# Fourteen modulation chunks as VectorE dot products, and the low halves that open the second layer's MLP cut in pieces

## The reference, cut to what matters

```
for layer in range(2):
    mod_x = silu(c) @ ada_w[layer] + ada_b[layer]        # 1024 -> 6144, for the tokens
    mod_c = silu(c_ctx) @ ada_w[layer] + ada_b[layer]    # the same for the context
    sh1, sc1, g1, sh2, sc2, g2 = split(mod_x, 6)
    ...mixer..., x = x + g1 * (mx @ w_out[layer])
    hx = rmsnorm(x, norm2_g[layer]) * (1 + sc2) + sh2
    x = x + g2 * (square(relu(hx @ w_mlp1[layer])) @ w_mlp2[layer])   # 1024 -> 4096 -> 1024
    if layer == 0: the same for ctx, with mod_c
```

## Time and profile before

| | |
|---|---|
| runs | 2018.05, 2015.6 and 2018.36 us, median 2018.05 |
| profiled execution | 2015.12 us by its own clock, of which the span of the profile is 2013.3 us |
| TensorE (PE) | 1929.2 us busy, 96% of the span |
| VectorE (DVE) | 754.5 us, 37% |
| ScalarE (ACT) | 625.2 us, 31% |
| GpSimd (POOL) | 392.5 us, 19% |
| MLP of l = 0, as the span counts | from 1261 to 1592 us |
| MLP of l = 1 | from 1815 us |

### The profile page before, as it was taken

How to read it: one execution, slowest core, us unless ns; L and a number is a source line. 1 busy time by engine, 2 the same in 40 slices (tenths; PEclk the granted TensorE clock), 3 DMA queues, 4 the chain that set the end, 5 groups by cost and what they waited for, 6 DMA issues and landing times.

```text
span 2013.3 us, 27741 instructions
## 1 busy us (share of the span) xinstructions
PE 1929.2 (96%) x11650; PEld 1396.9 (69%) x11650; DVE 754.5 (37%) x1241; ACT 625.2 (31%) x939; POOL 392.5 (19%) x205
## 2 busy tenths in 40 slices
PE   5999999999999999998999899999999999888998
PEld 2777786954444444446887657777777778678998
DVE  1625255632222222225343844222223535564333
ACT  2523113232222222213112534222333511545454
POOL 2000000110000000004002232333333210424664
PEclk9999999989999999998999999999999999999999
DMA  9469817559999999981323004444444223414451
GB/s 359 161 244 363 294 54 298 198 231 414 427 420 424 423 423 426 421 349 51 113 84 126 34 32 146 147 153 171 157 146 146 85 94 116 170 43 163 172 184 47
DMA packets 120215, 428.41 MB, mean 213 GB/s; under 512 B 5690, under 2 KB 23141, under 8 KB 107456
## 3 DMA queue, kind: packets, MB, share of 16 engines
q1 hardware_dynamic: 118016, 416.56, 53.7%
q0 software_dynamic: 2112, 10.57, 1.5%
HBM read 426.07 MB, written 1.05 MB: 212 GB/s over the span
## 4 chain that ended last, share of the span: by engine, by line
PE 64%; PEld 18%; issue 7%; DVE 4%; ACT 3%; POOL 2%; DMA 1%; PEldq 0%; DVEq 0%; POOLq 0%; SPq 0%; ACTq 0%
PE bank L532 62%; PEld bank L532 18%; PE bank L547 2%; DMA ring<-in_ada_w 1%; DVE H L1930 1%; DVE H_low L1937 0%; POOL arena L1845 0%; POOL arena L1844 0%; PEldq L511 0%; DVE arena L2450 0%; POOL arena L1849 0%; POOL arena_r L1885 0%; POOL arena L1847 0%; POOL arena L1850 0%; POOL ring_low L1871 0%
## 5 line engine op out<-in xcount | busy, mean ns | idle before, releaser
L532 PE MATMUL bank<-arena_r 128*128 128x512 f32 (+1 forms) x2304 | 634.3, 345 | 13.6 <-ACT arena_r L1351 5.4
L532 PE MATMUL bank<-arena_r,ring_low 128*128 128x512 f32 (+2 forms) x1920 | 597.2, 343 | 5.4 <-DVE H_low L1937 5.3
L532 PEld LDWEIGHTS bank<-arena_r 128*128 128x128 f32 x2304 | 404.3, 190 | 106.6 <-issue 48.4
L532 PEld LDWEIGHTS bank<-arena_r,ring_low 128*128 128x128 f32 (+1 forms) x1920 | 353.5, 189 | 51.4 <-issue 6.1
L532 PE MATMUL bank<-arena 128*128 128x64 bf16 (+8 forms) x2588 | 304.0, 282 | 26.8 <-DMA arena<-in_hy_filt_w 11.5
L532 PE MATMUL bank<-ring,arena 128*64 128x512 f32 x1024 | 278.2, 595 | 1.1 <-ACT arena L1531 0.7
L532 PEld LDWEIGHTS bank<-arena 128*128 128x128 bf16 (+4 forms) x2588 | 187.1, 131 | 129.6 <-issue 94.7
L532 PE MATMUL bank<-H_low,arena_r 128*128 128x512 f32 (+1 forms) x672 | 216.3, 339 | 0.0
L2508 DVE SCALAR_TENSOR_TENSOR X<-bank,mod,X 128x256 f32<-128x256 f32 x216 | 94.6, 479 | 316.9 <-PE bank L532 316.7
L1871 POOL TENSOR_TENSOR ring_low<-ring,arena_r 128x2048 fp32r<-128x2048 f32 x32 | 146.9, 4613 | 137.7 <-ACT arena_r L1721 70.1
L1365 ACT ACTIVATE arena<-bank 128x512 f32<-128x512 f32 (+2 forms) x106 | 51.2, 496 | 373.2 <-PE bank L532 373.0
(11 more groups left out here) (297 smaller groups left out, 1940.3 us busy)
## 6 DMA issues: line engine op xcount, KB each, us to landing
ring<-in_moe_w_gate SPq DMA_DIRECT2D x32, 2048.0 KB, 13.9
ring<-in_w_mlp SPq DMA_DIRECT2D x32, 2048.0 KB, 8.7
ring<-in_w_in SPq DMA_DIRECT2D x26, 2048.0 KB, 8.1
ring<-in_ada_w SPq DMA_DIRECT2D x24, 2048.0 KB, 11.9
ring<-in_moe_w_up SPq DMA_DIRECT2D x17, 2048.0 KB, 9.5
H<-in_moe_w_down SPq DMA_DIRECT2D x16, 2048.0 KB, 16.3
arena<-in_moe_w_up SPq DMA_DIRECT2D x15, 2048.0 KB, 9.6
ring<-in_moe_w_down SPq DMA_DIRECT2D x15, 2048.0 KB, 16.5
```

Of the source, the lines that this page charges most:

```text
L532: ins = nc.tensor.matmul(o, l, r, start=start, stop=stop, skip_group_check=True)
```

## The change

Part A is in the MLP of l = 0. The first step's pair of modulation chunks stays on TensorE. The other seven pairs, 42 blocks of 128 output columns, are computed on VectorE. Their weights come transposed (`ada_t_2`: 128 columns on the partitions, 1024 inputs along the free axis, 3 blocks to a chunk), and `CSIL` holds silu(c) and silu(c_ctx) spread over all partitions, 128 x 2048. It is brought by a GpSimd DMA, and ScalarE applies the silu behind step 0. For each block VectorE multiplies the 128x1024 weights by each of the two vectors and sums along the free axis into a column of `mod`: 12 instructions in a step, 84 in all. Three turns of four are gone, and the bias is added once behind the last step. TensorE now waits for `dots` between the hid phase and the W2 phase, and the W1 slot and both modulation slots are freed there together.

Part B is at the opening of l = 1's MLP. The second piece of W1's low half moves from GpSimd to VectorE, behind its second add. The high copy of W2 moves on ScalarE from behind the norm to between the squares of tiles 3 and 4. The low half of W2 is made in two pieces of 2048, the first ahead of the norm and the second behind it.

```diff
+                                if isinstance(i, int) and h == 0:
+                                    load(n, cols(T["ada_w_2"][1], q * ADA_COLS, ADA_COLS), as_cols(n, ADA_COLS), i * per)
+                                else:
+                                    load(n, rows(T["ada_t_2"], q * ADA_COLS, ADA_COLS), as_turned(n), i * per)
...
-                        chunk_used(3 if early else 1)
-                        n += 1
-                        if early:
-                            n += 2
-                        elif l == 0:
-                            for a in range(2):
-                                ada(n, 7 + i, 7, 2 * u + a, 4, ADA_COLS, turns)
-                                n += 1
+                        if l == 0 and not early:
+                            pe.wait_ge(S("dots"), 6 * j)
+                        chunk_used(1 if l else 3)
+                        n += 1 if l else 3
                         pe.wait_ge(S("w_split"), 9 + 8 * l + j + 1)
...
-                            if (l, u, nt) == (0, 1, 3):
-                                ada_turn(7 + i, 7, 0, 4, ADA_COLS)
+                            if (l, j, nt) == (0, 0, 3):
+                                ada_turn(7, 7, 0, 2, ADA_COLS)
...
                     square(k, W).then_inc(S("squares"), 1)
+                    if l and k == 3:
+                        act.wait_ge(full[(MLP1 + 1) % RING], arrived(MLP1 + 1))
+                        A_(W2h, slot(MLP1 + 1), ACT.Copy).then_inc(S("w_high"), 1)
...
+                        if l == 0 and isinstance(i, int) and u == 0:
+                            ada_rows(7, 7, 0, ADA_COLS)
+                            act.wait_ge(S("b2_in"), 16 * 5)
+                            A_(CSIL, CSIL, ACT.Silu).then_inc(S("silu_c"), 1)
...
-                low_w1(0, 0)
+                low_w1(0, 0, range(2 - l))
                 add_squares(4 + 2 * l, W)
                 phase_end(pool, f"l{l}_out")
+                if l == 0:
+                    bring(CSIL, T["c_all_2"].rearrange("p (a d) -> p a d", a=2), "b2_in")
...
                     add(t, ps[OUT_BANK[t]], 16).then_inc(S("w_out_added"), 1)
+                    if l and t == 1:
+                        dve.wait_ge(S("w_high"), 24 + 2)
+                        V.tensor_tensor(low(MLP1)[:, 2048:4096], slot(MLP1)[:, 2048:4096], W1h[:, 2048:4096].bitcast(F32), ALU.subtract)\
+                            .then_inc(S("w1_split"), 1)
...
+                if l:
+                    dve.wait_ge(S("w_high"), 24 + 3)
+                    low_w2(MLP1 + 1, 0, 2048)
                 norm(ncall, 1 + l, 1, (0, 1) if l == 0 else (0,))
...
+                        dotted = l == 0 and not (isinstance(i, int) and (i, u) == (0, 0))
+                        if dotted:
+                            dve.wait_ge(S("silu_c"), 2)
+                            dots(i, u, range(4))
                         dve.wait_ge(S("w_high"), 24 * l + (i * 2 + u) * 3 + 3)
                         n = mlp_chunks(l, u, 1, i)[0]
-                        V.tensor_tensor(low(n), slot(n), W2h.bitcast(F32), ALU.subtract).then_inc(S("w_split"), 1)
+                        low_w2(n, 2048 if l and isinstance(i, int) and (i, u) == (0, 0) else 0, 4096).then_inc(S("w_split"), 1)
+                        if dotted:
+                            dots(i, u, range(4, 6))
...
+                def dots(i, u, blocks):
+                    n0, turns = MLP0 + 4 * u + 1, i * 32
+                    for q in blocks:
+                        n = n0 + q // 3
+                        if q % 3 == 0:
+                            dve.wait_ge(full[n % RING], arrived(n) + turns)
+                        if q or not (isinstance(i, int) and (i, u) == (0, 1)):
+                            dve.wait_ge(S("dots"), i * 12 + u * 6 + q - 6)
+                        for c in range(2):
+                            d = V.scalar_tensor_tensor(CPROD[:, c, :], as_turned(n)[:, q % 3, :], 1.0, CSIL[:, c, :], ALU.mult, ALU.mult,
+                                                       accum_out=mod[:, 2, bass.ds(i * 12 + u * 6 + q, 1), c])
+                        d.then_inc(S("dots"), 1)
...
+                    dve.wait_ge(S("ada_out"), 2 + 8)
+                    dve.wait_ge(S("dots"), 42)
+                    lo = VOFF["ada_b2"][0] + 48
+                    link(V.tensor_tensor(mod[:, 2, 6:48, :], mod[:, 2, 6:48, :], bc(vecs[:, lo + 6:lo + 48].unsqueeze(2), [P, 42, 2]), ALU.add))
                     gains(2)
```

More of the change, by code:

```diff
@@ L252, in as_rows, with as_turned @@
             return slot(n).rearrange("p (k n) -> p k n", k=4)
+        def as_turned(n):
+            return slot(n)[:, 0:3 * D].rearrange("p (b d) -> p b d", b=3)
         E5 = 8328 + 3 * 4096
@@ L344, in _, with mlp_loads @@
                     load(first + 16 + j, cols(T["w_out_2"][l], j * 512, 512), as_cols(first + 16 + j))
-                with sp.Fori(0, 4) as i:
+                def mlp_loads(i):
                     n = mlp
@@ L357, in _ @@
                         n += 1
+                if l == 0:
+                    mlp_loads(0)
+                with sp.Fori(1 - l, 4) as i:
+                    mlp_loads(i)
             for a in range(4):
@@ L492, in build @@
         MLP_BANK = (4, 5, 2, 3)
+        CSIL, CPROD = A3(12288, 2, D), A3(22944, 2, D)
         W1h_cols, W2h_rows = W1h.rearrange("p (k n) -> p k n", k=KT), W2h.rearrange("p (k n) -> p k n", k=4)
@@ L873, in _ @@
                        "logits" if (tb, k) == (1, 7) else None)
-            pe.wait_ge(S("sw_zero"), 1)
+            pe.wait_ge(S("selected"), 1)
             pe.wait_ge(S("h_rest"), 4)
@@ L880, in _ @@
                 stat(2, k, L, CSQ)
-            pe.wait_ge(S("selected"), 1)
+            pe.wait_ge(S("selected"), 2)
             mm(ps[5][:, 0:NX], SLT, SELX[:, 0, :])
@@ L1742, in mlp_pair @@
                             high_w1(n)
[L1743 to L1746, removed]
+                        if not (l and isinstance(i, int) and u == 0):
+                            n, turns, chunks, back = mlp_chunks(l, u, 1, i)
+                            act.wait_ge(full[n % RING], arrived(n) + turns)
+                            act.wait_ge(used, n - back + 1 + chunks)
+                            A_(W2h, slot(n), ACT.Copy).then_inc(S("w_high"), 1)
                         for nt in range(4):
@@ L1852, in _ @@
                 pool.wait_ge(S("lgam"), l + 1)
-                pool.wait_ge(S("b2_in"), 16 * (4 + l))
+                pool.wait_ge(S("b2_in"), 16 * (4 + 2 * l))
                 head_args(0)
@@ L1864, in _, with low_w1 @@
                 phase_end(pool, f"l{l}_att")
-                def low_w1(i, u):
+                def low_w1(i, u, halves=range(2)):
                     n = mlp_chunks(l, u, 0, i)[0]
-                    for a in range(2):
+                    for a in halves:
                         s = slice(2048 * a, 2048 * (a + 1))
@@ L2526, in _, with low_w2 @@
                 phase_end(dve, f"l{l}_out")
+                def low_w2(n, a, b):
+                    return V.tensor_tensor(low(n)[:, a:b], slot(n)[:, a:b], W2h[:, a:b].bitcast(F32), ALU.subtract)
+                if l:
+                    dve.wait_ge(S("w_high"), 24 + 3)
+                    low_w2(MLP1 + 1, 0, 2048)
                 norm(ncall, 1 + l, 1, (0, 1) if l == 0 else (0,))
@@ L2538, in mlp_pair @@
                             add(t, ps[MLP_BANK[t % 4]], 40).then_inc(S("mlp_bank_free"), 1)
-                            if (l, u, t) == (0, 1, 4):
-                                take_chunk(2, 7 + i, 7, i * 12, 4, ADA_COLS)
+                            if l == 0 and not dotted and t == 4:
+                                take_chunk(2, 7, 7, 0, 2, ADA_COLS)
                             if l == 0 and closing and t in (2, 3):
@@ L2547, in mlp_pair @@
                                     i_.then_inc(full[(L1 + 1) % RING], 16)
-                with dve.Fori(0, 3) as i:
+                def dots(i, u, blocks):
[10 more added lines that the diff above has]
+                        d.then_inc(S("dots"), 1)
+                mlp_pair(0)
+                with dve.Fori(1, 3) as i:
                     mlp_pair(i)
@@ L2580, with spread @@
         arrays[name] = I[name]
+    def spread(v):
+        return np.broadcast_to(v.reshape(1, -1), (P, v.size))
+    arrays["ada_t_2"] = np.ascontiguousarray(I["ada_w_2"][1].T)
+    arrays["c_all_2"] = np.ascontiguousarray(spread(np.concatenate([I["c_2"].reshape(-1), I["c_ctx_2"].reshape(-1)])))
     arrays["wr"] = np.concatenate([I["moe_router_g_w"][0], I["moe_router_e_w"][0].transpose(1, 0, 2).reshape(D, NX)], axis=1)
```

18 lines of the change are left out of this document (7 added, 11 removed).

## The result

The changed kernel takes 2022.68 us (median of 20 runs), the kernel before 2018.09 us (20 runs): a ratio of 1.0027 with the interval 1.0018 to 1.0036. It is slower by 0.27%, about 5 us. The range held the time, but the forecast, no change with a lean to faster, did not hold.

A forecast was written before the change was run, and what follows sets the result against it. TensorE was taken to bound the kernel (89% of the chain). Part A −21.4 + 17.5 + 5.1 + 0.3 = +1.5 and part B −1.9 summed to −0.4 us: 2014.7 by profile, 2017.7 by median, given as 2017, range 2005 to 2028.

The forecast's parts named there:

- no change with a lean to faster: Whole kernel: 2017 us; chances 0.38 within 0.2% of before, 0.35 faster, 0.27 slower.
- What goes from TensorE, −21.4 us: MLP of l = 0: seven modulation pairs (19.7 us) and three turns (1.7 us) leave TensorE's list.
- the bias included that I put at +0.3: End of the MLP of l = 0: the bias over 84 columns costs some 0.3 us.
- The pause, 2.5 us a step, +17.5: Between hid and W2 phase, seven steps: TensorE waits for dots ending 24.6 us after hid phase start H; bounds 0 to 27.
- The rate of the dot products: VectorE, MLP of l = 0: 1222 ns per 128x1024 instruction, readout of the sum 0 to 160 ns.
- The half-rate rival: VectorE's dot instructions: with a sum they take twice the time, 2.29 us; +87 us, about 2105; chance 0.04.
- The clock, three falls, +5.1: Behind the new TensorE pauses in l = 0: clock falls three times in seven, 1.7 us each; bounds 0 to 11.9.
- The rival with a fall in every pause: MLP of l = 0: seven falls of 1.7 us, stall 2.8 to 3.3 us; about 2026 to 2030; chance 0.23.
- The ring: W1's slot in l = 0 comes free later, leaving 0.4 us of slack before the hid phase; costed at nothing.
- Part B, −1.9: Opening of l = 1's MLP: shorter first-step wait and no fall there, longer pause ahead of opening; −1.9 us (−4 to 0).
- VectorE's piece was charged with 0.4 us: Opening of l = 1's MLP: VectorE's piece may be held by GpSimd's, costing 0.4 us.

The follow-up runs named there:

- late_behind: Changed kernel, TensorE's wait for dots moved behind three W2 part tiles, VectorE's last four dot instructions held until GpSimd's third subtraction; 1993.10 us, 0.9876 of before.
- The kernel with one input: Changed kernel, each dot instruction replaced by a tensor-scalar sum over the weights alone, reading one SBUF input (different modulation); 1994.39 us, 0.9885 of before.
- filler: Changed kernel plus nine unused 128x512 matmuls on TensorE before its wait for dots, in steps 1 to 7 of l = 0; 2014.75 us, 0.9987 of before.
- drop1: Changed kernel with the last of a step's twelve dot instructions cut from 1024 to 64 columns; 2005.46 us, 0.9938 of before.
- the late wait: Also late_wait: changed kernel, TensorE waits for dots only behind the first two W2 part tiles; 1999.92 us, 0.9909 of before.
- part B alone: Part B put on the kernel before, modulation left as it was; 2016.59 us, 0.9995 of before.
- a_only: Changed kernel with part B taken back, so part A alone; 2025.24 us, 1.0036 of before.
- late_wait_2: Changed kernel, TensorE waits for dots only behind three W2 part tiles, nothing else; 1998.22 us, 0.9906 of before.

## Why the forecast went wrong, point by point

- *What goes from TensorE, −21.4 us.* In late_behind the stretch has neither pauses nor falls and is 22.4 us shorter than before, with the bias included that I put at +0.3. The term was 1.3 us too small.
- *The pause, 2.5 us a step, +17.5.* Measured 2.39 us, 16.7 in all. The place, the releaser, the three dot instructions that are held (1.10, 1.08 and 0.84 us, 3.0 in all, forecast 3 × 0.90) and their end at H + 24.6 are as forecast. The kernel with one input shows the cause.
- *The rate of the dot products.* 1.22 us and 0.08 for the readout. The half-rate rival falls: a sum with two float32 inputs in SBUF runs at the rate of the same operation without one. The Trainium skill ("Vector Engine (DVE) Microarchitecture Reference", section "7. Points that are easy to get wrong") says half; the measurement decides against it.
- *The clock, three falls, +5.1.* **This is the step that failed.** Six of seven pauses made the clock fall: 6 × 1.7 = 10.2 us, 5.1 more than charged. The forecast's 2017.7 by the median and 5.1 make 2022.8; 2022.68 was measured. That this agrees to 0.1 us is partly luck, since the smaller misses cancel: in the stretch the term for what goes was 1.3 us and the pause 0.8 us better than charged, 0.7 us are unexplained, and l = 1 gained 0.9 us where 1.9 were forecast. That the falls come of the pauses is shown by the filler (the same wait, the pause filled with nine matmuls, one fall), by drop1 (shorter pauses, no fall) and by the late wait. What they cost is shown by the sum: 335.22 + 16.7 + 10.2 = 362.1 us for the stretch against 362.87 measured. I had two pauses of 2.29 us, one with a fall and one without, and split the difference. The mechanism of this step was right and its size wrong. The rival with a fall in every pause was nearest, with its stall too long; it said itself that with seven falls it decides from a stall of 2.2 us on, and the stall was 2.39.
- *The ring.* No hid phase waited for W1, neither in the changed kernel nor with the late wait: costed at nothing, and nothing it was. The prediction calls the transposed chunks smaller; they have 1536 KB, as the modulation chunks of before have.
- *Part B, −1.9.* The pauses came out as forecast: 3.46 (3.5 forecast) and a fall ahead of the opening, 1.11 and no fall ahead of the W2 phase. From the instruction shortly before the projection to the end of the span, part B alone gained 1.6 us, and the changed kernel 1.8 us against a_only. So the term was about right. One part of it was too kind: VectorE's piece was charged with 0.4 us and held for 3.9, TensorE then stood 0.36 us for a bank in the projection, and the pause for the sums kept 0.41 us. By the medians alone the gain can't be told from nothing. The changed kernel's l = 1 as a whole is only 0.9 us shorter than before, since it takes 0.8 us more ahead of that instruction, in code that part B leaves as it was.

Open: why the clock stayed at 1.00 behind the first pause of the changed kernel (2.19 us) and of a_only (2.27 us) and fell behind others of 2.2 us. Early in l = 1 stands a pause of 2.50 to 2.57 us in ten of the twelve kernels; the clock stayed up behind it in nine and fell in late_wait_2 (2.57 us). Behind the 3.46 us ahead of l = 1's opening it fell in eight of nine kernels and stayed at 1.00 in late_wait. Length alone does not decide, and no run here shows what does.

## What to carry to other kernels

Before an engine's free time is filled, look at which engine waits for the result: here nobody needed the dot products before the layer's end, and only the place of a wait, there to free a buffer, put them on the critical path. Move such a wait to where the work is surely done, and let the engine whose result is needed next have the shared port first. Price a new pause of TensorE with the clock, and with a range: in this loop 1.4 us cost 1.4 us and 2.4 us mostly cost about 4, while elsewhere in the same kernels 2.5 us mostly cost no more than its length.

## What the runs showed of the hardware

The granted clock against the length of the pause, at the same place of the same loop: none of 7 pauses of 1.0 to 1.5 us made it fall to 0.50, one of 7 of 1.1 to 1.9 us did (behind 1.83), and 12 of 14 of 2.2 to 2.6 us. Each of these falls lasted 3.4 us. Elsewhere in the same kernels pauses of 2.50 to 2.57 us made it fall once in ten, and pauses of 3.46 us eight times in nine. Filling the pause with matmuls whose result nobody uses kept the clock in six of seven steps and made the kernel faster. On VectorE a dot product over 128x1024 in float32, both inputs in SBUF, takes 1.22 us alone, 0.08 us for the readout of the sum, and up to 2.33 us when a GpSimd subtraction over 128x512 meets it.
